# Delta-rule stage: the output-gate products are spread between the key and query products, and ACT takes its squares ahead of its copy

## What is computed

```python
proj = rmsnorm_2(h, norm_mix_g) @ w_in            # columns: pool | q | k | v | z | b, a
qkv  = silu(causal_dwconv(concat(q, k, v), conv_w))
qf, kf = l2norm(q heads), l2norm(k heads)         # unit norm over the 128 of a head
L    = strict lower(k_beta @ k^T * decay)         # key products, per chunk
T    = inverse(eye + L)                           # unit lower triangular
attn = lower(q @ k^T * decay)                     # query products
# recurrence over the chunks with T, attn, k, v gives o
o = rmsnorm(o) * o_norm_g * silu(z)               # z: the output gate
y = concat(pool mixer output, o) @ w_out
```

## Time and profile before

| | before |
|---|---|
| median of 3 runs | 2834.44 us |
| profiled execution | 2836.63 us |
| its span, first to last instruction | 2834.8 us |
| TensorE (PE) busy | 2704.4 us, 95% |
| VectorE (DVE) busy | 1249.0 us, 44% |
| ScalarE (ACT) busy | 526.0 us, 19% |
| GpSimd (POOL) busy | 171.0 us, 6% |

### The profile page before, as it was taken

One profiled execution on the slowest core, in us unless ns is written; L12 is line 12 of the kernel. 1 busy time (PEld: TensorE's weight loads), 2 busy tenths in 40 slices (PEclk: granted clock), 3 DMA queues, 4 the chain that ended last, 5 costly groups with the idle time before them and its releaser, 6 DMA issues.

```text
span 2834.8 us, 32087 instructions
## 1 busy us (share of the span) xinstructions
PE 2704.4 (95%) x12682; PEld 1801.3 (64%) x12682; DVE 1249.0 (44%) x2310; ACT 526.0 (19%) x874; POOL 171.0 (6%) x140
## 2 busy tenths in 40 slices
PE   7999999999899999999799999989989999999997
PEld 3688888887544444685343333334486777888886
DVE  4255666564444444545311111155373335654644
ACT  2122122122233333211100000031312103100001
POOL 1122221120000000231000000000000000000000
PEclk9999999999999999999899999999999999999999
DMA  9522121111111121235599999932102331333330
GB/s 357 197 59 59 52 59 52 44 30 37 45 53 45 46 59 45 75 90 214 226 409 409 409 409 409 407 93 74 30 1 81 116 86 37 83 90 90 89 90 30
DMA packets 327673, 374.57 MB, mean 132 GB/s; under 512 B 10033, under 2 KB 273030, under 8 KB 324230
## 3 DMA queue, kind: packets, MB, share of 16 engines
q1 hardware_dynamic: 327286, 371.93, 38.3%
q10 hardware_dynamic: 272, 1.05, 0.1%
HBM read 370.85 MB, written 2.10 MB: 132 GB/s over the span
## 4 chain that ended last, share of the span: by engine, by line
PE 91%; DVE 4%; DVEq 2%; DMA 1%; ACT 1%; SPq 1%; issue 1%; ACTq 0%
PE psum L1650 31%; PE psum L1952 12%; PE psum L1381 8%; PE psum L2108 6%; PE psum L720 3%; PE psum L1118 2%; PE psum L1837 2%; PE psum L815 2%; PE psum L705 2%; PE psum L728 2%; PE psum L2639 2%; PE psum L1878 2%; PE psum L1308 2%; PE psum L1360 1%; PE psum L1337 1%; PE psum L2721 1%
## 5 line engine op out<-in xcount | busy, mean ns | idle before, releaser
L1650 PE MATMUL psum<-arena 128*128 128x256 f32 x4144 | 909.0, 379 | 1.9 <-DVEq L1673 1.2
L1650 PEld LDWEIGHTS psum<-arena 128*128 128x128 f32 x4144 | 779.9, 189 | 117.4 <-issue 5.3
L1952 PE MATMUL psum<-arena 128*64 128x512 f32 x1536 | 347.6, 597 | 3.0 <-issue 2.1
L1952 PEld LDWEIGHTS psum<-arena 128*64 128x64 f32 x1536 | 105.0, 136 | 217.4 <-issue 214.3
L1381 PE MATMUL psum<-arena 128*128 128x512 f32 x512 | 233.1, 597 | 0.0
L2108 PE MATMUL psum<-arena 128*128 128x512 f32 (+1 forms) x448 | 168.8, 534 | 0.0
L1682 DVE TENSOR_TENSOR arena<-psum,arena 128x256 f32<-128x256 f32 x66 | 28.1, 425 | 313.3 <-ACT arena L1695 192.7
L1381 PEld LDWEIGHTS psum<-arena 128*128 128x128 f32 x512 | 92.4, 189 | 104.1 <-issue 104.1
L1883 DVE SCALAR_TENSOR_TENSOR arena<-psum,arena 128x512 f32<-128x512 f32 x64 | 48.0, 750 | 246.4 <-PE psum L1878 245.8
L2108 PEld LDWEIGHTS psum<-arena 128*128 128x128 f32 x448 | 85.4, 191 | 82.9 <-issue 79.4
L1657 POOL TENSOR_TENSOR arena<-arena 128x512 f32<-128x512 f32 x34 | 47.3, 1391 | 1121.3 <-DMA arena<-in_w_in 655.0
(11 more groups left out here) (379 smaller groups left out, 3212.7 us busy)
## 6 DMA issues: line engine op xcount, KB each, us to landing
arena<-in_w_gate SPq DMA_DIRECT2D x64, 1024.0 KB, 18.4
arena<-in_w_up SPq DMA_DIRECT2D x64, 1024.0 KB, 16.1
arena<-in_w_down SPq DMA_DIRECT2D x64, 1024.0 KB, 18.0
arena<-in_w_in SPq DMA_DIRECT2D x120, 512.0 KB, 4.0
arena<-in_ada_w SPq DMA_DIRECT2D x24, 1024.0 KB, 7.0
arena<-in_w_up SPq DMA_DIRECT2D x32, 512.0 KB, 5.4
arena<-in_w_down SPq DMA_DIRECT2D x32, 512.0 KB, 4.9
arena<-in_w_out SPq DMA_DIRECT2D x16, 512.0 KB, 3.8
```

Source lines behind the costliest of these rows:

```text
L1650: mm = pe.matmul(psum[:, base + b, c * HALF:(c + 1) * HALF], w, v, start=(first and q == 0 and m in (0, 2, 3, 4)), stop=(last and q == KC ...
L1952: mm = pe.matmul(psum[64 * e:64 * e + 64, bank + n, :], tokens(e, 2 * q + k), w[:, k, 512 * n:512 * n + 512], start=(q == 0 and k == 0), s ...
```

## The change

ACT's two squares of a round move ahead of the copy of that round's v block. The four z products leave `pe_in2` and are put between the parts of `pe_dn`. The key products go to banks 4, 5, 2, 3 (before: 2, 3, 4, 5) and the query products to 6, 7, 4, 5 (before: 6, 7, 0, 1). ACT no longer copies z out to apply silu later: one silu reads the bank directly, behind ACT's other work of `act_dn`. Waits are set for the new users of the banks: `pe_left` of heads 0 and 1 at level 0 waits for "inverse" 3 and 4, and the first two `pe_turn_kv` for the third and fourth z output.

```diff
@@ pe_in2
-            for u in range(4):
-                if u == 0:
-                    pe.wait_ge(sem("pooled"), 4)
-                if u >= 2:
-                    pe.wait_ge(sem("z_out"), u - 1)
-                product(pe, "z2", 0, u, hm, u % 2)
@@ act_in2
             for n in range(4):
-                act_qkv_copy(act, 8 + n)
                 for m in (2 * n, 2 * n + 1):
                     act.activation(l2_sq[m % 2], qkv[:, L2_ORDER[m], :], ACT.Square).then_inc(sem("l2_squares"), 1)
+                act_qkv_copy(act, 8 + n)
                 act_l2_root(act, 2 * n)
                 act_l2_root(act, 2 * n + 1)
-            for u in range(4):
-                done(act, "z2", 0, u)
-                act.activation(z_silu[:, u, :], psum[:, u % 2, :], ACT.Copy).then_inc(sem("z_out"), 1)
@@
+        KEY_GRAM, QUERY_GRAM = (4, 5, 2, 3), (6, 7, 4, 5)
@@ pe_left
             if l == 0:
-                if h >= 2:
+                if h < 2:
+                    pe.wait_ge(sem("inverse"), h + 3)
+                else:
                     pe.wait_ge(sem("inverse"), DNH + h - 1)
@@ pe_turn_kv
-            if n >= 2:
+            if n < 2:
+                pe.wait_ge(sem("z_out"), n + 3)
+            else:
                 pe.wait_ge(sem("kv_out"), n - 1)
@@ pe_dn
+            pe.wait_ge(sem("l2_done"), DNH)
+            pe.wait_ge(sem("pool_out"), 4)
             for h in range(DNH):
-                pe.wait_ge(sem("l2_done"), h + 1)
-                if h == 0:
+                if h == 2:
                     pe.wait_ge(sem("qkv_out"), 12)
-                    pe.wait_ge(sem("pool_out"), 4)
-                pe_gram(pe, h, 4, 2 + h)
+                pe_gram(pe, h, 4, KEY_GRAM[h])
+            pe.wait_ge(sem("pooled"), 4)
+            product(pe, "z2", 0, 0, hm, 0)
             pe.wait_ge(sem("l2_done"), 8)
-            pe.wait_ge(sem("z_out"), 4)
-            for h in range(DNH):
-                pe_gram(pe, h, 0, (6, 7, 0, 1)[h])
-
-            for h in range(DNH):
-                pe_left(pe, 0, h)
+            pe_gram(pe, 0, 0, QUERY_GRAM[0])
+            pe_gram(pe, 1, 0, QUERY_GRAM[1])
+            pe_left(pe, 0, 0)
+            pe_left(pe, 0, 1)
+            product(pe, "z2", 0, 1, hm, 1)
+            pe_left(pe, 0, 2)
+            pe_left(pe, 0, 3)
+            pe_gram(pe, 2, 0, QUERY_GRAM[2])
+            pe_gram(pe, 3, 0, QUERY_GRAM[3])
+            for u in (2, 3):
+                pe.wait_ge(sem("z_out"), u - 1)
+                product(pe, "z2", 0, u, hm, u % 2)
             await_once(pe, "queries_out")
@@ act_dn
             for n in range(8, 12):
                 act_qkv_silu(act, n)
-            act.drain()
             for u in range(4):
-                act.activation(z_silu[:, u, :], z_silu[:, u, :], ACT.Silu).then_inc(sem("z_out"), 1)
+                done(act, "z2", 0, u)
+                act.activation(z_silu[:, u, :], psum[:, u % 2, :], ACT.Silu).then_inc(sem("z_out"), 1)
@@ dve_dn
-                dve.tensor_tensor(head(d_c, h), head(d_c, h), tiles(2 + h), ALU.mult)
+                dve.tensor_tensor(head(d_c, h), head(d_c, h), tiles(KEY_GRAM[h]), ALU.mult)
@@
-                dve.tensor_tensor(head(d_b, h), head(d_b, h), tiles((6, 7, 0, 1)[h]), ALU.mult)
+                dve.tensor_tensor(head(d_b, h), head(d_b, h), tiles(QUERY_GRAM[h]), ALU.mult)
@@
-            dve.wait_ge(sem("z_out"), 8)
+            dve.wait_ge(sem("z_out"), 4)
```

## The result

The changed kernel is faster. Its median over 6 runs is 2820.73 us (2816.23 to 2823.91); the kernel before, now with 6 runs, has 2837.28 (2832.34 to 2838.01). The ratio is 0.9946 with an interval of 0.9935 to 0.9957: 15.3 us less, 12.2 to 18.4. The forecast was 17.9 us less and 2816.5. The median lies inside the range of 2812.5 to 2821.5, but the ratio applied to the six-run median of before gives 0.9946 x 2837.28 = 2822.0, above the range. So the direction and the mechanism held, while the base and the size of the gain were off; what follows says by which terms.

The account below looks back on a forecast made before the run. PE's list and its waits for ACT and DVE were taken as the bound. 14.95 us up to level 1 plus 2.96 us of clock made 17.9 us, from 2834.44 to 2816.5 us, range 2812.5 to 2821.5.

Parts of the forecast that it names:

- rival A: Level-0 transposes: new PE waits of 0.35 and 1.9 us bring the clock down, costing 1.7 us; 2818.2 us, chance 0.28.
- What bounds: Whole kernel: PE is 91% of the chain that ended last, so only shortening its list or waits moves the end.
- E: The end of the last v product, from which the prediction counts the times of both lists up to level 1.
- Part 1: v rounds: squares ahead of the copy cut each from 10.07 to 8.60 us; the first three give 4.41 us.
- Part 2: From the last v product's end to level 1: 40.2 us instead of 50.74, so 10.5 us sooner.
- Part 3: Level 1's first piece: full clock instead of a low one, 4.44 us for 7.40, so 2.96 us won.
- The rule on transposes: Level-0 transposes: if they don't count as PE-busy, PE looks idle from 13.8 to 16.95 us and a low clock follows.
- Part 4: The rest: removed ACT copies and z weights cost or gain nothing; everything behind level 1 shifts as a block.
- C: DVE's side is 3 us longer, the wait for "inverse" 4 becomes 5 us, the clock falls; 2821.2 us, chance 0.05.
- B: v rounds: ACT's squares still come late and rounds keep 10.07 us; gain 12.0 us, 2822.4 us, chance 0.04.
- D: `row_exp` is held back by work on z, PE stands at "inverse" 4 and loses 26.1 us; 2842.6 us, chance 0.01.

Follow-up runs that it names:

- e2: Changed kernel with ACT's copy of v put back ahead of its two squares in each v round; ratio 0.9965, 9.9 us less than the kernel before.
- e7: Changed kernel with two more matmuls, result unused, between the level-0 transposes of heads 0 and 1, filling PE's 1.7 us wait; 2819.89 us, ratio 0.9939.
- e4: Changed kernel again, no edit, with its own profile; 2821.82 us, ratio 0.9950 to the kernel before.
- e1: Kernel before with one edit: ACT's two squares ahead of its copy in each v round; 2829.46 us, ratio 0.9976.
- e5: Changed kernel with ACT's `row_exp` moved behind the four silus of v; 2824.58 us, ratio 0.9956 to the kernel before.
- e3: Changed kernel with z products 1 to 3 each one place earlier, so that no PE wait is left; 2815.39 us, ratio 0.9922 to the kernel before.
- e9: Changed kernel a third time, no edit, with its own profile; 2822.05 us, ratio 0.9953 to the kernel before.

## Why the prediction was right and wrong

**The miss in one sum.** The ratio puts the changed kernel at 2822.0 beside a base of 2837.28; I said 2816.5. Of these 5.5 us, 2.8 are the base, a median of three executions taken for the kernel's time; 1.4 are rival A, to which I gave too small a chance; 1.2 are open. The first two are the steps that failed. The mechanism of the 17.9 us was right, and 17.82 were measured in the stage where the clock stayed up.

**What bounds.** Right. PE's list was the chain and its waits were the gain. In the stage the rounds (4.4 us), the way from E to level 1 (10.5) and the clock in level 1 (2.9) account for all of it.

**Part 1, the squares.** Right: 8.59 us a round instead of 10.07, in round 0 too, where the squares ended just ahead of the product. Alone it gave 6.4 us in the stage and 6.8 by ratio (4.3 to 9.4), for 5.9 forecast.

**Part 2, the two lists from E.** Right to 0.05 us at its end: level 1 at E + 40.24 for E + 40.2. `row_exp` and DVE's start came at E + 5.11 and E + 7.05 for 5.15 and 7.1. The transposes of heads 0 and 1 started at E + 14.13 and E + 16.47 for 14.15 and 16.5. The profile gives the waits as 0.18 and 1.71 where I had 0.35 and 1.9: it counts them from modelled ends, 0.16 behind the pitch, so the times agree. Nothing cost anything where I had put nothing: no wait of PE on z banks, z weights or `queries_out`.

**Part 3, the clock in level 1.** Right: 4.50 us for 4.44, in each of the six profiles.

**Rival A, the clock behind the new waits: the mis-sized term of the gain.** Its price was right (1.7 us, each time). Its chance was not: I gave it 0.28 and it came in five profiles of six. So the likeliest case was not the forecast of 17.9 us but A, with 16.1. The step that failed was to set the four waits of 1.21 us, which had left the clock alone, against two waits of 2.02 and 2.08 us with a low stretch behind them, and to take the side of the former. The rows were also read too simply. The 2.08 did not stand alone: 3.7 us ahead of it, in the same profile of before, stands a wait of 1.71, as long as the one in question. And a wait of 2.48 us a little later left the clock up:

```profile
727.73 1.16 PE L815 MATMUL psum<-arena 128*128 128x128 f32 x8 [1.71 <-DVEq L860]
...
747.63 0.49 PE L905 MATMUL psum<-arena 128*128 128x128 f32 x2 [2.48 <-DVEq L898]
```

```profile
747.60:751.00 3.40, 3.37 (x26) 2.98 (x26) 0.00 (x0) 0.39 (x1) 0.00 (x0) 1.00 0.00 0
```

One profile can't give such a chance. The first block is the same in all versions, and in the first profile of the changed kernel the same waits are followed by the full clock:

```profile
692.31 1.23 PE L815 MATMUL psum<-arena 128*128 128x128 f32 x8 [2.02 <-DVEq L860]
...
730.60 1.31 PE L870 MATMUL psum<-arena 128*128 128x128 f32 x10 [2.07 <-DVEq L860]
```

```profile
692.30:695.70 3.40, 3.39 (x27) 3.34 (x28) 2.13 (x6) 0.89 (x2) 0.00 (x0) 1.00 0.03 8
731.70:735.10 3.40, 3.40 (x10) 1.56 (x9) 0.10 (x1) 1.36 (x3) 0.00 (x0) 1.00 0.02 5
746.20:749.60 3.40, 3.40 (x18) 3.40 (x18) 0.00 (x0) 0.00 (x0) 0.00 (x0) 0.50 0.00 0
```

There the low clock stands behind the wait of 2.48 us instead (the last row). Over all 14 profiles the clock is low behind both the 2.02 and the 2.08 in six, and behind the 2.48 in the other eight. The length of a wait alone doesn't decide.

The two new waits lie only 0.63 us apart, with four transposes between them: 1.89 us of waiting together. In e2, where one wait of 1.29 stands alone, the clock stayed up in its profile; in e7, with 0.18 left, too. These are one profile each, and so they don't show that such a wait is safe.

**The rule on transposes.** The prediction weighs a sentence of the Trainium skill ("TensorE: Matmul & The Clock Gate", Part 4: PE-mode transpose), that a transpose does not count as PE-busy in the way a matmul does. By it PE would look idle across both waits and the transposes between them, and what the six profiles show fits that as well as it fits the waits alone. But the full clock (1.00) behind 36 transposes in a row speaks against it, and no run here tells the two apart; that the transposes played a part stays open.

**Part 4 and the base.** The block behind level 1 did shift as one, but its length isn't constant: from the second left product of level 1 to the end of the span it takes 762.2 to 762.6 us in seven profiles and 764.1 to 764.6 in the seven others, over all versions. So my "shifts as a block" left out 2 us that come and go from one execution to the next. In e4 most of the difference can be seen at the end of the cross-attention, where the same three waits are followed by 5.40 us instead of 3.71 for the same eight records; both kernels have these waits:

```profile
2347.86 0.44 PE L2787 MATMUL psum<-arena 128*128 128x128 f32 x2 [1.03 <-DVE arena L2840]
2348.58 0.44 PE L2787 MATMUL psum<-arena 128*128 128x128 f32 x2 [0.28 <-DVE arena L2840]
2349.49 5.40 PE L2799 MATMUL psum<-arena 128*128 128x512 f32 x8 [0.47 <-ACT arena L2817]
```

In the first profile of the changed kernel:

```profile
2345.78 3.71 PE L2799 MATMUL psum<-arena 128*128 128x512 f32 x8 [0.47 <-ACT arena L2817]
```

Four of the six profiles of the changed kernel are of the longer kind; of before there is only one, of the shorter kind. So I can't say whether the change makes this more frequent or whether it is as frequent before. With A at five in six, and that alone, the expected gain is 17.8 - 1.4 = 16.4 us; the three measured gains (15.3, 14.2, 13.3) have intervals that hold it, yet all lie below. The remaining 1 to 3 us are not settled.

The base was too low as well: the median of three executions was 2834.44 and that of six 2837.28, which alone moves the forecast to 2819.4, and with A to 2821.1. The medians of before beside the experiments are 2837.28 (16 executions), 2837.54 (9) and 2837.65 (7), so 2834.44 was a low draw. The profiled execution lay above it, at 2836.63, and with it as the base A would have given 2820.4.

The upper end of the range doesn't follow from its own words. It was to hold A and C with the spread of 3.0 us above; A with it is 2821.2, but C is 2824.2, and the range ended at 2821.5.

**The other rivals.** B fell (e1). C fell: DVE's side was as built to 0.05 us, not 3 longer. D was tested in small by e5: over 3.50 us the dependence is one to one and has no slack, which supports its price, though no run delayed `row_exp` by 26 us. The order on ACT excluded it. The chance of 0.98 for faster by over 0.2% came true: the interval ends at 12.2 us, and 5.7 is the bound.

## What to carry to other kernels

Where two engines work by turns, write down both lists from one common event, with pitches from the trace; here that gave the new stage to 0.05 us.

Take the base from more than three executions, or set the profiled one beside it: here the base was the largest part of the miss.

Treat every wait that is left as a risk for the clock. Here two waits of 1.89 us together were followed by a low stretch in five profiles of six, and one of 2.02 us in six of fourteen. So price the low stretch in, add waits that lie close together, and don't take the chance from one profile: look at all rows of similar length, those with the full clock behind them too.

A wait that can be covered by work that has to be done anyway, as z product 1 in e3, is worth its own length and that risk.

## What the runs showed that I had not expected

- Filling a 1.71 us wait of PE with two matmuls whose result nobody reads went with a median 2.2 us lower and a spread of 1.7 instead of 7.1 us (e7 beside e9, five runs each, ratio intervals overlapping).
- The same program with the same waits, to 0.01 us, gets a low clock of 3.4 us behind them in one execution and not in another (five of six). In the first block, alike in all versions, the low clock stands behind waits of 2.02 and 2.08 us in six profiles and behind one of 2.48 us in the other eight.
- Six executions of the changed kernel cover 7.7 us (2816.23 to 2823.91), while its stage differs by 1.7 us over six profiles. Ahead of it, the end of the product before the first norm sums lies between 1981.2 and 1985.3 us in 14 profiles of programs that are alike up to the rounds.
